# A fused two-block transformer kernel: the first output product's tiles are kept without the full heads' factor

## The reference, cut to what matters

```
mixed = concat([rms_norm(out_a, group_norm_a), rms_norm(out_b, group_norm_b)]) @ w_out
x = x + rms_norm(mixed, norm_mix_post)
h = rms_norm(x, norm_ffn_pre)
f = (silu(h @ w_gate) * (h @ w_up)) @ w_down
# rms_norm(y, g) = y * rsqrt(mean(y * y) + EPS) * g,  EPS = 1e-6
```

## Time and profile before

| what | us |
|---|---|
| median of 3 plain runs | 1161.18 (1160.88 to 1161.55) |
| the profiled execution | 1164.91 |
| its span, first to last instruction | 1163.1 |
| PE busy in the span | 1133.3 (97%) |
| DVE busy | 650.2 (56%) |
| ACT busy | 503.0 (43%) |

### The profile page before, as it was taken

How to read it: one execution, slowest core, us unless ns; L and a number is a source line. 1 busy time by engine, 2 the same in 40 slices (tenths; PEclk the granted TensorE clock), 3 DMA queues, 4 the chain that set the end, 5 groups by cost and what they waited for, 6 DMA issues and landing times.

```text
span 1163.1 us, 15505 instructions
## 1 busy us (share of the span) xinstructions
PE 1133.3 (97%) x5560; PEld 936.3 (80%) x5560; DVE 650.2 (56%) x1085; ACT 503.0 (43%) x859; POOL 124.5 (11%) x143
## 2 busy tenths in 40 slices
PE   8999989999999999999999999999999999999997
PEld 6788767898888888888898887787888888888886
DVE  5888896966444444333378588563544444433333
ACT  5788885544223223222255458453322322332321
POOL 1476743000000000000000004200000000000000
PEclk8999999999999999999999999999999999999999
DMA  7321202213222222233223220032322222222312
GB/s 266 109 73 51 59 19 108 92 55 140 95 104 90 94 102 96 92 108 109 96 77 109 91 76 16 19 109 73 111 92 105 93 95 100 95 103 93 106 55 73
DMA packets 32515, 106.20 MB, mean 91 GB/s; under 512 B 4048, under 2 KB 6736, under 8 KB 32336
## 3 DMA queue, kind: packets, MB, share of 16 engines
q1 hardware_dynamic: 31712, 104.60, 25.5%
q10 hardware_dynamic: 752, 0.92, 0.3%
HBM read 100.78 MB, written 2.10 MB: 88 GB/s over the span
## 4 chain that ended last, share of the span: by engine, by line
PE 86%; DVE 6%; ACT 3%; POOL 2%; issue 2%; DMA 1%; ACTq 0%; SPq 0%; DVEq 0%; POOLq 0%
PE bank L502 24%; PE bank L504 24%; PE bank L503 23%; PE bank L1015 1%; PE bank L1005 1%; DVE wl L423 1%; PE bank L1088 1%; PE bank L963 1%; PE bank L964 1%; PE bank L965 1%; POOL pr L1335 1%; PE bank L1090 1%; PE bank L1089 1%; PE bank L2004 1%; PE bank L2002 1%
## 5 line engine op out<-in xcount | busy, mean ns | idle before, releaser
L423 DVE TENSOR_TENSOR wl<-raw,wh 128x1024 fp32r<-128x1024 f32 x181 | 223.9, 1238 | 299.3 <-ACT wh L415 299.2
L415 ACT ACTIVATE wh<-raw 128x1024 fp32r<-128x1024 f32 x181 | 191.1, 1057 | 420.3 <-PE bank L504 275.0
L502 PE MATMUL bank<-hh,wh 128*128 128x512 f32 x872 | 344.8, 395 | 4.3 <-DVE hl L1486 2.7
L504 PE MATMUL bank<-hh,wl 128*128 128x512 f32 x872 | 340.8, 391 | 0.0
L503 PE MATMUL bank<-hl,wh 128*128 128x512 f32 x872 | 340.6, 391 | 0.0
L502 PEld LDWEIGHTS bank<-hh,wh 128*128 128x128 f32 x872 | 164.4, 188 | 41.7 <-issue 4.8
L503 PEld LDWEIGHTS bank<-hl,wh 128*128 128x128 f32 x872 | 164.5, 189 | 35.3 <-issue 1.7
L504 PEld LDWEIGHTS bank<-hh,wl 128*128 128x128 f32 x872 | 164.2, 188 | 34.8
L504 PE MATMUL bank<-gh,wl 128*128 128x512 f32 x308 | 121.7, 395 | 0.0
L502 PE MATMUL bank<-gh,wh 128*128 128x512 f32 x308 | 121.7, 395 | 0.0
L503 PE MATMUL bank<-gl,wh 128*128 128x512 f32 x308 | 121.7, 395 | 0.0
(11 more groups left out here) (245 smaller groups left out, 1635.3 us busy)
## 6 DMA issues: line engine op xcount, KB each, us to landing
raw<-weights SPq DMA_DIRECT2D x181, 512.0 KB, 3.2
xres<-x_t SPq DMA_DIRECT2D x8, 512.0 KB, 7.6
sw<-ta SPq DMA_DIRECT2D x36, 64.0 KB, 2.0
out_t<-final SPq DMA_DIRECT2D x6, 256.0 KB, 2.5
rope<-angles SPq DMA_DIRECT2D x1, 1024.0 KB, 10.8
sw<-ta ACTq DMA_DIRECT2D x4, 64.0 KB, 3.1
wp<-pool_weights ACTq DMA_DIRECT2D x1, 256.0 KB, 2.6
out_t<-final ACTq DMA_DIRECT2D x1, 256.0 KB, 2.4
```

The lines of the kernel that those rows point to most:

```text
L415: act.activation(wh[:, j, :, :], raw[:, j, :, :], ACT.Copy).then_inc(high_split, 1)
L423: v.tensor_tensor(wl[:, j, :, :], raw[:, j, :, :], wh[:, j, :, :].bitcast(F32), ALU.subtract)\
L502: pe.matmul(bank[:, :], wh[:, slot, b, :], ah[:, k, :], start=first and n == 0, stop=False)
L504: ins = pe.matmul(bank[:, :], wl[:, slot, b, :], ah[:, k, :], start=False, stop=last and n == len(blocks) - 1)
```

## The change

With A and B the two banks' contents and a and b the factors, the kernel before keeps m = A*a + B*b. Now it keeps m' = A + B*(b/a), that is m divided by a. The norm that follows removes a factor per token but for its eps: rsqrt(mean(m*m) + EPS) * m equals rsqrt(mean(m'*m') + EPS/(a*a)) * m', and 1/(a*a) is sum/512 + EPS. This eps by token is put into acc ahead of the squares, as a share on each of 128 partitions.

In the instructions:

- ACT computes only the logarithm for group A; `rstd` then holds it. DVE gets a new instruction that reads the bank of the sum and writes acc. n_ga.ready now counts 2, one from each, and PE waits for both ahead of unit 2.
- For group B, ACT's logarithm is followed by a DVE subtraction (log of B less log of A), and then by ACT's exponential, which gives b/a in `sq`.
- `vec_mix` makes one product instead of two (window times sq). `vec_mix_add` adds the full bank to it, straight from PSUM, and it is now this instruction that signals the banks as read.
- The first square is added to acc and no longer copied into it. ACT waits for bank_read where it waited for mixed_there. The logarithms of the two halves' norms are taken without the eps column.

```diff
 (PE, pe_out1)
-            pe.wait_ge(n_ga.ready, 1)
+            pe.wait_ge(n_ga.ready, 2)
 (ACT, at the tick behind the sum of group A)
-                act_rstd(act, n_ga, ring_bank("sum", 1), rstd, 512)
+                act.wait_ge(n_ga.summed, 1)
+                act.activation(rstd[:, :], ring_bank("sum", 1)[:, :], ACT.Ln, bias=col("eps"), scale=1.0 / 512)\
+                    .then_inc(n_ga.ready, 1)
 (ACT, act_tail1)
-            act_rstd(act, n_gb, banks[6], sq, 512)
+            act.wait_ge(n_gb.summed, 1)
+            act.activation(sq[:, :], banks[6][:, :], ACT.Ln, bias=col("eps"), scale=1.0 / 512).then_inc(ln_b, 1)
+            act.wait_ge(ln_ratio, 1)
+            act.activation(sq[:, :], sq[:, :], ACT.Exp, scale=-0.5).then_inc(n_gb.ready, 1)
 (DVE, vec_mix and vec_mix_add)
-            v.tensor_tensor(ta[:, d % 2, n], full[:, n], rstd[:, n], ALU.mult).then_inc(mixed_parts, 1)
-            v.tensor_tensor(tb[:, d % 2, n], window[:, n], sq[:, n], ALU.mult).then_inc(bank_read, 1)
+            v.tensor_tensor(ta[:, d % 2, n], window[:, n], sq[:, n], ALU.mult).then_inc(mixed_parts, 1)
             v.wait_ge(mixed_parts, u + 1)
-            v.wait_ge(bank_read, TILE0["out1"] + u + 1)
-            v.tensor_tensor(mixed1[:, d, n], ta[:, d % 2, n], tb[:, d % 2, n], ALU.add).then_inc(mixed_there, 1)
+            full, _ = out_banks(u)
+            v.tensor_tensor(mixed1[:, d, n], full[:, n], ta[:, d % 2, n], ALU.add).then_inc(bank_read, 1)
 (DVE, vec_take1)
-            v.wait_ge(n_ga.ready, 1)
+            v.wait_ge(n_ga.ready, 2)
+            v.wait_ge(ln_b, 1)
+            v.tensor_tensor(sq[:, :], sq[:, :], rstd[:, :], ALU.subtract).then_inc(ln_ratio, 1)
             v.wait_ge(n_gb.ready, 1)
             for u in range(5):
                 vec_mix(v, u)
-                if u >= 1:
+                if u == 1:
+                    v.wait_ge(n_mp.squared, 1)
+                    v.tensor_tensor(acc[:, :], acc[:, :], sw[:, 0, :], ALU.add).then_inc(n_mp.added, 1)
+                elif u > 1:
                     add_square(v, n_mp, u - 1, acc)
 (ACT, act_half_square; act_take1 alike)
-            act.wait_ge(mixed_there, UNITS.index((d, half)) + 1)
+            act.wait_ge(bank_read, TILE0["out1"] + UNITS.index((d, half)) + 1)
 (ACT, act_half_rstd of the two halves, now called with eps=False)
+                link(act, "a", act.activation(rstd[:, n], bank[:, n], ACT.Ln, scale=1.0 / D))
 (DVE, its whole program)
             for t in range(TICK0, TICKS):
                 vec_tick(v, t)
+            v.wait_ge(n_ga.summed, 1)
+            v.tensor_scalar(acc[:, :], ring_bank("sum", 1)[:, :], EPS_SHARE[0], EPS_SHARE[1], ALU.mult, ALU.add).then_inc(n_ga.ready, 1)
             vec_mix_low(v, 7)
             vec_take1(v)
```

More of the change, by code:

```diff
@@ L1419, in act_tail1 @@
             act_mix_high(act, 7)
-            act_rstd(act, n_gb, banks[6], sq, 512)
-        mixed_there = sem("mixed1_there")
+            act.wait_ge(n_gb.summed, 1)
+            act.activation(sq[:, :], banks[6][:, :], ACT.Ln, bias=col("eps"), scale=1.0 / 512).then_inc(ln_b, 1)
+            act.wait_ge(ln_ratio, 1)
+            act.activation(sq[:, :], sq[:, :], ACT.Exp, scale=-0.5).then_inc(n_gb.ready, 1)
         mixed_parts = sem("mixed1_parts")
+        ln_b = sem("groupB_ln")
+        ln_ratio = sem("group_ratio_ln")
+        EPS_SHARE = (EPS * D / P / (4 * P), EPS * EPS * D / P)
         first_half = sem("out1_first_halves")
@@ L1429, in vec_mix @@
             n = tokens(half)
-            full, window = out_banks(u)
+            _, window = out_banks(u)
             if half == 0:
@@ L1557, in act_half_square, with act_half_rstd @@
             act.activation(sw[:, d % 2, n], mixed1[:, d, n], ACT.Square).then_inc(norm.squared, 1)
-        def act_half_rstd(act, norm, half, bank):
+        def act_half_rstd(act, norm, half, bank, eps=True):
             n = HALVES[half]
             act.wait_ge(norm.summed, 1)
-            link(act, "a", act.activation(rstd[:, n], bank[:, n], ACT.Ln, bias=col("eps"), scale=1.0 / D))
+            if eps:
+                link(act, "a", act.activation(rstd[:, n], bank[:, n], ACT.Ln, bias=col("eps"), scale=1.0 / D))
+            else:
+                link(act, "a", act.activation(rstd[:, n], bank[:, n], ACT.Ln, scale=1.0 / D))
             act.activation(rstd[:, n], rstd[:, n], ACT.Exp, scale=-0.5).then_inc(norm.ready, 1)
@@ L1574, in act_take1 @@
                 act_split(act, c0 + d + RING)
-                act.wait_ge(mixed_there, d + 1)
+                act.wait_ge(bank_read, TILE0["out1"] + d + 1)
                 act_square(act, n_mp, d, mixed1[:, d, :])
@@ L1578, in act_take1 @@
                 act_half_square(act, d, 0)
-            act_half_rstd(act, n_mh[0], 0, banks[6])
+            act_half_rstd(act, n_mh[0], 0, banks[6], eps=False)
             act_split(act, g0 + 1)
@@ L1592, in act_take1 @@
             act_half_h(act, join1, 6, 0)
-            act_half_rstd(act, n_mh[1], 1, banks[7])
+            act_half_rstd(act, n_mh[1], 1, banks[7], eps=False)
             act_half_h(act, join1, 7, 0)
```

## The result

| | median us | lowest to highest | executions |
|---|---|---|---|
| kernel before | 1161.57 | 1160.88 to 1163.46 | 16 |
| changed kernel | 1163.68 | 1162.73 to 1164.94 | 16 |

The ratio is 1.0018 with a 95% interval of 1.0011 to 1.0025: the change makes the kernel 2.1 us slower. That is just under the 0.2% that the prediction took for the smallest difference a measurement can tell; sixteen executions of each do tell it from no change. 1162.8 was forecast.

The account below looks back on a forecast made before the run. The prediction took PE as the bound in the output product and VectorE between 217.7 and 229.6 us. Terms +2.26 +0.39 -1.01 = +1.64 us on plain runs at 1161.18 gave 1162.8 us, range 1161.0 to 1164.5.

Parts of the forecast that it names:

- Unit 2: In front of unit 2, PE waits for VectorE's new write of acc: 2.26 us of new idle, bounds 2.0 to 2.3.
- Two hand-overs: Ahead of unit 2: new VectorE instruction starts 0.08 us before its predecessor ends; PE starts 0.05 us after it ends.
- Unit 3: In front of unit 3, VectorE's subtraction delays ScalarE's exponential and so PE: 0.39 us, bounds 0.25 to 0.7.
- Units 0 to 7 at nothing: Output product, units 0 to 7: VectorE loses eight products, but PE doesn't wait there; worth 0.
- The join: Units 8 to 10: one VectorE instruction fewer in each, so PE gains 1.01 us; bounds 0.67 and 1.3.
- Product to first scaling: Sign of being right: unit 8's product to the first scaling takes 0.86 us instead of 1.20.
- The wait for the fourth low half: Sign of being right: this PE wait ends some 1.0 us earlier, counted from unit 8's product.
- The clock: Rival: the 2.2 us PE gap in front of unit 2 halves the clock, +3.0 us, 1165.8 us; chance 8%.
- The argument against it: Against a clock fall: from 180 to 183 us PE was busy only 1.53 of 3.0 us at clock 1.00.
- The sum: Whole kernel: +2.26 +0.39 -1.01 = +1.64 us, giving 1162.8 us, 0.14% slower.
- the wait did bite: Rival said the wait in front of unit 2 costs nothing, leaving -0.6 us, 1160.6 us; chance 5%.
- the join did give its microsecond: Rival said ScalarE's hand-overs set the pace in units 8 to 10, no gain: +2.65, 1163.8 us; chance 12%.

Follow-up runs that it names:

- e5_wait_alone: Kernel before plus only the new wait in front of unit 2 (VectorE reads the bank into acc, value unused): median 1165.16 us, ratio 1.0028.
- e9_longer_filled: e8_longer with 18 extra products on PE ahead of the wait in front of unit 2: median 1165.75 us, ratio 1.0033.
- e4_filled: Changed kernel with nine extra products on PE ahead of its wait in front of unit 2: median 1163.37 us, ratio 1.0018.
- e8_longer: Changed kernel with three more VectorE reads of the bank ahead of the write of acc, lengthening PE's idle stretch: median 1168.15 us, ratio 1.0054.
- e2_log: Changed kernel with PE's unit 3 waiting for group B's logarithm instead of the exponential: median 1163.96 us, ratio 1.0019.
- e7_back_early: e3_both with VectorE's remaining product done twice in units 0 to 7: median 1160.65 us, ratio 0.9994.
- e3_both: Changed kernel with VectorE writing acc ahead of head 15's addition, and PE's unit 3 waiting for group B's logarithm: median 1160.16 us, ratio 0.9990.
- e3_again: The kernel of e3_both run once more without edits: median 1160.91 us, ratio 0.9995.
- e6_back_late: e3_both with VectorE's remaining product done twice in units 8 to 10: median 1161.23 us, ratio 1.0000.

## Why the prediction was right, point by point

**Unit 2: mechanism right, term too small.** 2.26 us was forecast, with bounds of 2.0 to 2.3; 2.57 and 2.56 were measured in the two profiles and 2.57 in e5_wait_alone (2.92 less 0.35), outside the bounds. Place, cause and end of the wait are as forecast, and so is the instruction's duration (0.69 against 0.68). Two hand-overs were mis-sized. The forecast let L2211 start 0.08 us ahead of the end of L1157, as VectorE does between the units' products; it started 0.04 behind it (182.68 + 0.68 = 183.36, then 183.40), +0.12. L1157 works on 64 partitions, the upper half in head 15, and L2211 on all. The trace of before had a price for just this. Behind L1157 of an even head, which writes the lower half, the next instruction starts about 0.60 us after it, and behind that of an odd head, the upper half, about 0.72 after it; so it is in each of the first thirteen heads, within 0.01 us:

```profile
114.75 0.67 DVE L1157 TENSOR_TENSOR xres<-bank,xres 64x512 f32<-64x512 f32 x1
115.34 0.67 DVE L1114 TENSOR_SCALAR_CACHE_REDUCE pr<-bank 128x512 f32<-128x512 f32 x1
...
122.67 0.68 DVE L1157 TENSOR_TENSOR xres<-bank,xres 64x512 f32<-64x512 f32 x1
123.38 0.69 DVE L1114 TENSOR_SCALAR_CACHE_REDUCE pr<-bank 128x512 f32<-128x512 f32 x1
```

The Trainium skill (VectorE: DVE Perf Modes, section "Two Vector instructions with no wait between them") has a rule by which an instruction waits for all earlier ones when its input or output starts in another quarter of the partitions than the last one before it in the same memory; these pairs agree with it. And PE started 0.26 us behind the end of L2211 (184.09 to 184.35), where 0.05 was taken from other hand-overs: +0.21. This part goes with PE having idled: behind the same instruction PE started 0.05 after its end in e9_longer_filled and in e4_filled, where it had products to do, and 0.26 in e8_longer. Why it is long isn't settled; at unit 3 PE followed 0.10 behind ScalarE, and at the join it followed 0.06 behind VectorE after 1.12 us of idle time.

**Unit 3: right.** 0.39 forecast, 0.43 measured; e2_log takes 0.42 of it away. This is its place in the changed kernel:

```profile
194.30 0.63 ACT L1425 ACTIVATE sq<-sq 128x512 f32<-128x512 f32 x1 [0.83 <-DVE sq L1515]
...
195.03 0.47 PE L963 MATMUL bank<-mix_h,wh 128*128 128x512 f32 x1 [0.19 <-issue]
```

Only 0.19 us of it is idle time in the profile and it is put down to issue. The product ahead is shown as 0.40 us long, but in a full stream the next one follows it after 0.23, so PE starts 0.36 late; the other 0.08 is the exposed weight load (first spacing 0.31 instead of 0.23). Looking for it in the list of waits one would miss it.

**Units 0 to 7 at nothing: right.** Shown by e7_back_early, 0.07 us for eight instructions.

**The join: right.** -1.01 forecast with bounds of -0.67 to -1.3; -1.16 between before and e3_both, -1.02 with e3_again. e6_back_late shows that it is those three instructions. VectorE in the changed kernel:

```profile
218.84 0.42 DVE L1444 TENSOR_TENSOR ta<-bank,sq 128x256 f32<-128x256 f32 x1 [2.65 <-PE bank L965]
219.30 0.42 DVE L1451 TENSOR_TENSOR mixed<-bank,ta 128x256 f32<-128x256 f32 x1
219.64 0.48 DVE L1477 SCALAR_TENSOR_TENSOR ta<-mixed,cols,rstd 128x256 f32<-128x256 f32 x1
```

Product to first scaling is 0.80 us (forecast 0.86, before 1.20). Before, PE had three waits at the join, the two of the earlier trace rows and between them this one, for the low part of a weight chunk:

```profile
226.35 0.39 PE L1088 MATMUL bank<-hh,wh 128*128 128x256 f32 x1 [0.50 <-DVE wl L423]
```

In the changed kernel the first is gone, this one stays and the last is shorter by 0.3:

```profile
226.76 0.38 PE L1088 MATMUL bank<-hh,wh 128*128 128x256 f32 x1 [0.49 <-DVE wl L423]
229.68 0.39 PE L1088 MATMUL bank<-hh,wh 128*128 128x256 f32 x1 [0.79 <-DVE hl L1489]
```

The wait for the fourth low half ends 10.84 us behind unit 8's product, and before it was 11.92: 1.08 us earlier, where some 1.0 was forecast. The prediction doesn't name the middle wait; it moves along with the rest of VectorE's work and so cost the sum nothing.

**The clock: the rival under-rated.** It was given 8% as a case of its own, at +3.0 us. It is no separate case but a part of the executions: it happened in the first profile and not in the second, at 1.57 us, half the price, since the fall lasted 3.4 us and not 6.4. The argument against it (180 to 183 us, PE busy 1.53 of 3.0 at full clock) took one execution for a rule. No fall came at that stretch in any profile without the new wait, but another sparse stretch, at 149 us, had the clock at 1.00 in the first profiles of both kernels and at 0.50 in five others, so one profile doesn't say what a sparse stretch does.

**The sum.** +1.64 forecast; without a fall the profile gives +1.76 (979.71 less 977.95), that is +2.57 + 0.43 and, by difference, -1.2 from the join. The plain medians give +2.1 and +2.4. The difference of 0.3 to 0.7 us would be a fall of 1.57 us in a fifth to less than a half of the executions; that share is worked out and not counted, and the intervals of both ratios (1.3 to 2.9 us and 1.4 to 3.5 us) take in +1.76 without it. Of the 0.9 us between the 1162.8 that was forecast and the 1163.68 measured, 0.4 is the base: the median of before was 1161.18 over three runs and is 1161.57 over sixteen. So the path is as forecast, but that the total came so near is in part luck: the join's gain, the wait's size and the clock's share were each missed by a few tenths, two upwards and one down.

The other two rivals on record: the wait did bite, and the join did give its microsecond.

## What to carry to other kernels

Where an instruction stands in its engine's queue decides its cost: the same read of a bank cost 2.57 us behind a waiting instruction and nothing 2.6 us earlier, in front of it. When a stage's factor is split over two engines, let the next writer of the bank wait for the last read of the bank, not for the last step of the computation. Compare profiles by the distance between two marks around the change, since what the clock does before it can be larger than the change.

## What the runs showed of the hardware

- The granted clock falls to 0.50 in some executions at sparse places: of 14 profiles one shows it at 11.4 to 17.8 us (that of before), two near 42 us, five near 149 us, and two at the new idle stretch: one of the four with a gap of 2.3 us (two of the changed kernel, e2_log, e5_wait_alone) and the only one with 4.5 us. In four it fell nowhere while PE still had work, and in none twice.
- At the new idle stretch a fall cost 1.57 us where it lasted 3.4 us and at least 2.38 where it lasted 6.7 us or more. Elsewhere the price differs by place: the last value product starts at 181.1 to 181.7 us in the six profiles without an earlier fall, at 181.8 to 182.1 in the five with the one near 149 us, and at 183.23 and 183.85 in the two with the one near 42.
- A VectorE instruction on all 128 partitions started 0.03 us behind the end of the one ahead where that one had worked on the upper 64 partitions, and 0.07 ahead of its end where it had worked on the lower 64.
- GpSimd's addition of 128x256 took 1.51 and 2.49 us beside VectorE's, and held up one VectorE instruction each time by 0.5 us.
